# Attention of a two-layer hybrid backbone: values, gate and scores in halves of TensorE's array, channel by token

## The chip, the cores and the metric

One NeuronCore of a Trainium2 chip runs one program. The metric is the device time of one execution in microseconds, the median of several runs.

## The reference

A latent stream of 1024 tokens (8 tiles of 128) and a context of 256 tokens (2 tiles), both 1024 channels wide, in float32, pass two layers. A layer projects the modulated, normalised input into groups of channels, mixes each group in its own way, joins them through one output projection, and ends with routed experts. What the change touches:

```python
def spatial_gating(u, g, w_sgu, b_sgu):
    u = jax.nn.gelu(u, approximate=False)
    v = layer_norm(jax.nn.gelu(g, approximate=False))
    vh = v.reshape(b, n // SGU_CHUNK, SGU_CHUNK, N_SGU_HEADS, SGU_HEAD)
    mixed = jnp.einsum('hpq,bcqhd->bcphd', w_sgu, vh) + b_sgu.T[None, None, :, :, None]
    return u * mixed.reshape(b, n, GROUP_W)
...
    s_loc = jnp.einsum('bnikgd,bnjkd->bnkgij', qb, kw).astype(jnp.float32) * scale
    s_ctx = jnp.einsum('bnikgd,bckd->bnkgic', qb, kc).astype(jnp.float32) * scale
    probs = jax.nn.softmax(jnp.concatenate([s_loc, s_ctx, sink_l], axis=-1), axis=-1)
    o = (jnp.einsum('bnkgij,bnjkd->bnikgd', probs[..., :n_loc].astype(v.dtype), vw)
         + jnp.einsum('bnkgic,bckd->bnikgd', probs[..., n_loc:n_loc + n_ctx].astype(vc.dtype), vc))
...
    return jnp.concatenate([y_four, y_attn, y_pool, y_sgu], axis=-1) @ w_out
...
        x = layer_norm(RES_ALPHA * x + g1 * y, ln1_g[layer], ln1_b[layer])
        h2 = modulate(x, sh2, sc2)
```

There are 4 query heads of 64 channels on 2 key and value heads, and 4 gate heads of 64 channels. A tile of 128 queries sees three blocks of 128 keys (masked to +-128 tokens) and the 256 keys of the context; context tiles see the context alone. Each head has a sink logit in its softmax. `h2` goes to a router of 36 columns and to the experts. Layer 1 leaves the context's own output out.

## The kernel before

A layer runs in stages: `project_first` or `project_again` (input projection of 10 tiles, modulation vectors beside it), a transform stage (Fourier group and the like), `attend`, and `route_and_experts`. Tensors in SBUF written by one stage are read by the next: `qT` and `kT` channel by token, `v_tok`, `u_tok` and `sgu_v` token by channel, `four_tok` (in fact channel by token here) and `poolT` channel by token.

`attend` runs over its tiles as a software pipeline: in step t, tile t is attended, tile t-1 projected and tile t-2 routed. On TensorE (L1366 on, function `step`) the order of a step is: scores of pair 0 (two heads of one key head); the heads of tile t-1 turned from token by channel (`heads_tok`) to channel by token, 4 transposes (L1331), which ScalarE copies to `mixT` (L1245); first half of the projection of t-1 (512 of the 1024 output columns, 8 matmuls over 1024 channels, L1320); the probabilities of pair 0 turned, 10 transposes (L1290), copied by ScalarE to `probsT`; scores of pair 1; `h2` of t-2 turned, 8 transposes (L1347, L1350); second half of the projection; router of t-2 (L1360), whose result lies in the bank of `head_out`; values of pair 0 (L1305); probabilities of pair 1 turned; gate (L1311); values of pair 1.

A head of scores multiplies `q_head`, 128 rows of which the 64 of the other key head are zero, by 384 local keys (L1269) and 256 context keys (L1270). GpSimd makes `q_head` (L1085) by multiplying `qT` with a constant of ones and zeros, `K_KV`; it also copies the rows of `four_tok` and `poolT` into `mixT` (L1089, L1091), and computes the power for the norms (`norm_power`), the gain and bias behind the first norm (L1075, L1078) and the modulation of `h2` (L1099, L1101), each of 1024 elements per row.

Values have the turned probabilities as the stationary operand and 64 columns of `v_tok` moving, so `head_out` is token by channel; the gate has `w_sguT` stationary and 64 columns of `sgu_v` moving:

```python
mm = nc.tensor.matmul(O[:, 0, h * HD:(h + 1) * HD], pT[:, i, j, :], v, start=j == js[0], stop=j == 4)
...
nc.tensor.matmul(O[:, 1, h * HD:(h + 1) * HD], ws[:, h, :], sg[:, h * HD:(h + 1) * HD], start=True, stop=True)
```

VectorE masks scores and takes their maxima (`maxima`), normalises `h2` of t-2, copies it turned into `h2T` (L1180, L1182), adds the residual of t-1 once both halves of the projection are there (L1193, L1195), normalises that, and in `heads` adds `b_sgu`, multiplies by `u` (L1158) and divides the attention by its denominators (L1159), which are one number per token and so one per row. ScalarE takes the exponentials with their sums, copies turned tiles, and copies the router's logits (L1252). SyncE issues the stage's loads in the order of its code (`small_in` counts `b_sgu`, `w_sguT` and the two parts of `w_router`; TensorE waits for all four ahead of values of tile 0) and stores `h2`.

In the projection stages, the group u and g is 8 matmuls with `hT` stationary and 512 columns of `w_in` moving into `bankA`; ScalarE's gelu writes `u_tok` and `sgu_v`.

## Time and profile before

| | us |
|---|---|
| median of 3 runs | 2843.64 (2838.64 to 2847.23) |
| the profiled execution, its own time | 2844.69 |
| its span in the profile | 2842.5 |
| TensorE busy | 2454.1 (86%) |
| VectorE, ScalarE, GpSimd busy | 852.5 (30%), 437.3 (15%), 514.4 (18%) |
| attention, layer 0 (10 tiles) | 376.0 to 733.6 |
| attention, layer 1 (8 tiles) | 1757.4 to 2048.0 |
| input projection, layer 0 | 50 to 316 |
| mean granted clock of TensorE | 0.918 of full |

Times are microseconds from the start of the span. A matmul in float32 leaves two rows in the trace, a transpose one. Busy times of TensorE come with a modelled end: the start of the next row tells how long one really occupied the engine.

### The profile page before, as it was taken

To read this page: it belongs to the slowest core of one execution; us is meant where nothing else is said; L and a number is where in the kernel's file an instruction comes from. 1 tells how busy PE (TensorE), PEld (TensorE's weight loads), DVE (VectorE), ACT (ScalarE), POOL (GpSimd) and SP (SyncE) were. 2 spreads that over 40 slices of the span, in tenths; PEclk is the share of its full clock that TensorE was granted. 3 is DMA by queue.
4 is the path that set the end of the run, shared out by engine and by line. 5 is a ranking of instruction groups with operands and counts; after the bars stand their busy time and mean duration, and the time that the engine had idled before them with its cause. 6 is when DMAs were issued, how large, how long until landed. Compare 5 with 4: busy or idle time off the path is not lost. (4 is left out here: it accounts for less than half of the span.)

```text
span 2842.5 us, 38989 instructions
## 1 busy us (share of the span) xinstructions
PE 2454.1 (86%) x14774; PEld 1686.9 (59%) x14774; DVE 852.5 (30%) x2043; ACT 437.3 (15%) x1052; POOL 514.4 (18%) x691
## 2 busy tenths in 40 slices
PE   5999889998389999999967997999659999999960
PEld 3788556665266666666635784666346666666630
DVE  1232625543611111111107665454531111111107
ACT  0011122221001111111101112222001111111112
POOL 0000114334011111111110102234101111111116
PEclk7999889988589999999988998999769999999985
DMA  9444320001369999997534103000059999999953
GB/s 352 165 141 174 113 102 16 15 15 45 130 257 388 396 392 387 388 395 302 207 113 150 44 31 134 30 15 23 15 208 384 386 386 394 389 384 384 373 198 137
DMA packets 130588, 608.21 MB, mean 214 GB/s; under 512 B 21216, under 2 KB 23776, under 8 KB 112080
## 3 DMA queue, kind: packets, MB, share of 16 engines
q1 hardware_dynamic: 112048, 569.35, 51.6%
q0 software_dynamic: 17312, 37.79, 3.6%
q8 instruction: 50, 0.82, 0.1%
q14 instruction: 26, 0.21, 0.0%
q10 hardware_dynamic: 1152, 0.03, 0.0%
HBM read 612.52 MB, written 42.83 MB: 231 GB/s over the span
## 5 line engine op out<-in xcount | busy, mean ns | idle before, releaser
L1829 PEld LDWEIGHTS gate_up<-room,w_gate_up 128*128 128x128 f32 x4736 | 534.5, 193 | 32.3 <-issue 32.3
L1829 PE MATMUL gate_up<-room,w_gate_up 128*128 128x128 f32 x4736 | 541.6, 277 | 3.1 <-DVE room L1741 3.1
L1320 PE MATMUL proj<-w_out,mixT 128*128 128x512 f32 x576 | 261.7, 608 | 13.1 <-ACT mixT L1245 11.6
L1838 PE MATMUL down<-w_down,room 128*128 128x512 f32 x592 | 263.9, 599 | 0.0
L1846 PE MATMUL gate_up_short<-w_gate_up,room 128*64 128x512 f32 x1184 | 262.2, 595 | 0.0
L1750 DVE TENSOR_TENSOR room<-room,gate_up 128x128 f32<-128x128 f32 x148 | 42.6, 288 | 613.5 <-ACT room L1769 613.5
L1320 PEld LDWEIGHTS proj<-w_out,mixT 128*128 128x128 f32 x576 | 109.3, 195 | 142.7 <-issue 130.9
L1846 PEld LDWEIGHTS gate_up_short<-w_gate_up,room 128*64 128x64 f32 x1184 | 81.7, 137 | 175.9 <-issue 175.9
L1838 PEld LDWEIGHTS down<-w_down,room 128*128 128x128 f32 x592 | 109.4, 190 | 126.4 <-issue 123.9
L1753 DVE TENSOR_TENSOR room<-room,gate_up_short 128x256 f32<-128x256 f32 x37 | 15.6, 421 | 508.8 <-ACT room L1775 508.8
L1496 POOL COPY rows_idx<-slot_token 128x1 int32 (+1 forms) x80 | 14.6, 183 | 831.8 <-PE rows_turned L1816 729.7
L1859 PE MATMUL down<-w_down,room 128*64 128x512 f32 x592 | 135.2, 598 | 12.2 <-ACT room L1777 12.2
L1769 ACT ACTIVATE room<-gate_up 128x128 f32<-128x128 f32 x148 | 41.0, 277 | 519.8 <-PE gate_up L1829 519.8
L1816 PE MATMUL rows_turned<-consts,rows 128*128 128x128 f32 (+1 forms) x608 | 93.1, 286 | 17.7 <-DMA rows<-h_rows,rows_idx 17.7
L1816 PEld LDWEIGHTS rows_turned<-consts,rows 128*128 128x128 f32 (+1 forms) x608 | 77.1, 197 | 52.5 <-issue 48.0
L1741 DVE COPY room<-rows_turned 128x512 f32<-128x512 f32 (+1 forms) x152 | 78.2, 556 | 61.0 <-PE rows_turned L1816 61.0
L1305 PE MATMUL head_out<-v_tok,probsT 128*128 128x64 f32 (+1 forms) x672 | 89.8, 293 | 6.5 <-ACT logits L1252 6.5
L1499 POOL DMA_INDIRECT rows<-h_rows,rows_idx x80 | 80.9, 1012 | 71.7 <-POOL rows_idx L1496 50.1
L1305 PEld LDWEIGHTS head_out<-v_tok,probsT 128*128 128x128 f32 x672 | 86.6, 209 | 8.8 <-issue 8.6
L1859 PEld LDWEIGHTS down<-w_down,room 128*64 128x64 f32 x592 | 40.5, 136 | 81.3 <-issue 81.3
L467 PE MATMUL bankA<-w_in,hT 128*128 128x512 f32 x160 | 74.3, 619 | 15.9 <-ACT hT L412 15.9
L1773 ACT ACTIVATE room<-down 128x512 f32<-128x512 f32 x74 | 44.2, 597 | 267.0 <-PE down L1838 267.0
(322 smaller groups left out, 3039.6 us busy)
## 6 DMA issues: line engine op xcount, KB each, us to landing
w_gate_up<-in_w_exp_gate SPq DMA_DIRECT2D x74, 2048.0 KB, 8.8
w_gate_up<-in_w_exp_up SPq DMA_DIRECT2D x74, 2048.0 KB, 13.4
w_down<-in_w_exp_down SPq DMA_DIRECT2D x74, 2048.0 KB
ada_w<-in_w_ada SPq DMA_DIRECT2D x48, 1024.0 KB, 7.0
h_rows<-h SPq DMA_DIRECT2D x18, 512.0 KB, 2.6
w_out<-in_w_out SPq DMA_DIRECT2D x2, 4096.0 KB, 16.3
w_in<-in_w_in SPq DMA_DIRECT2D x2, 3072.0 KB, 16.6
xn<-expert_rows SPq DMA_DIRECT2D x10, 512.0 KB, 4.0
```

What stands on the lines that cost most here:

```text
L467: i = nc.tensor.matmul(out, lhsT(k), rhs(k), start=k == 0, stop=k == KT - 1)
L1305: mm = nc.tensor.matmul(O[:, 0, h * HD:(h + 1) * HD], pT[:, i, j, :], v, start=j == js[0], stop=j == 4)
L1320: mm = nc.tensor.matmul(Y[:, half, :], ys[1 - q][:, j, :], wo[:, k, half * 512:(half + 1) * 512], start=j == 0, stop=j == KT - 1)
L1499: pool.indirect_dma_start(xg[q][rows, :], None, g.h2[:, :], bass.IndirectOffsetOnAxis(ap=idx[q][rows, 0:1], axis=0), bounds_check=NT * P - ...
L1741: c = nc.vector.tensor_copy(xT[q][:, 4 * h:4 * h + 4, :], T[:, 4 * h:4 * h + 4, 0:P if q == 0 else HP])
L1750: nc.vector.tensor_tensor(hid[:, j, :], silu[:, j % 2, :], H[j % 2][:, 1, :], ALU.mult).then_inc(hid_done, 1)
L1773: nc.scalar.activation(yo[:, h * 512:(h + 1) * 512], Y[:, h, :], ACT.Copy).then_inc(y_done, 1)
L1816: tr = nc.tensor.transpose(T[:, k, 0:rows], xg[q][0:rows, k::KT], g.k[0:rows, K_ID:K_ID + rows])
L1829: mm = nc.tensor.matmul(H[j % 2][:, o, :], wgu[0][:, o, k, j * P:(j + 1) * P], xT[0][:, k, :], start=k == 0, stop=k == KT - 1)
L1838: mm = nc.tensor.matmul(Y[:, h, :], hid[:, j, :], wd[0][:, j, h * 512:(h + 1) * 512], start=j == 0, stop=j == JT - 1)
L1846: mm = nc.tensor.matmul(Hs[c * HP:(c + 1) * HP, :, :], xT[1][:, k, :], wgu[1][:, :, k, c * 2 * P:(c + 1) * 2 * P], start=k == 0, stop=k == ...
L1859: mm = nc.tensor.matmul(Y[h * HP:(h + 1) * HP, 0, :], hidT_s[:, j % 2, j // 2 * HP:(j // 2 + 1) * HP], wd[1][:, j, h * 512:(h + 1) * 512], ...
```

## The change

- **Values and gate, channel by token.** `v_tok` and `sgu_v` are now the stationary operands (64 columns of the array) and turned probabilities and `w_sguT` move, 128 columns. The result of a key head or of an even gate head goes to partitions 0 to 63 of `head_out`, that of the other to 64 to 127. Nothing turns the heads any more. Of the row of four blocks of `head_out`, 0 and 1 hold the two pairs, 2 and 3 first the gate and then the denominators.
- **Denominators as rows.** They now vary along the free axis, so GpSimd makes four diagonal matrices from the reciprocals (`den_diag`, `diagonals`), TensorE multiplies ones by them (`spread_den`), ScalarE copies that to `den_rows` and VectorE multiplies (`heads`).
- **Pairs.** A pair is now one query head of each key head (`sink`, `neg_max` and so on take every second head). The host orders rows of `w_out` to fit.
- **Scores in row halves.** Queries and keys of a key head are its own 64 rows of `qT` and `kT`; there is no `q_head` and no `K_KV`. A head's columns are 384 local and 128 "near" context keys into `scores`, and 128 "far" context keys into `scores_far`, in the order near 0, far 1, near 1, far 0, with a wait for far 1 ahead of far 0. The maxima take 512 and 128 columns of each head.
- **Projection.** It reads `four_tok` and `poolT` where they are, so `mixT` holds gate and attention rows alone; the waits for the gate and the attention rows stand ahead of their matmuls within the first half.
- **Residual in halves.** VectorE multiplies, adds and takes the statistics of columns 0 to 511 behind the first half of the projection, of the others behind the second.
- **Order.** On TensorE the gate comes ahead of the second half of the projection, `h2` is turned behind the probabilities of pair 1, and the router is last, into one of the two `turn` banks; which of the two banks each turning takes comes from a table. The loops over tiles are written out. SyncE's loads are in another order, `b_sgu` as rows in four loads, and `small_in` counts seven loads.
- **u, channel by token.** In the projection stages the 256 columns of u are 2 x 8 matmuls with `w_in` stationary and `hT` moving (128 columns), g is 8 of 256 columns, and gelu writes `uT`.

TensorE, one middle step of `attend`, before, from the turning of the heads on (the scores of pair 0 that stand ahead of it are the same four rows as those of pair 1; `x8` here is 8 matmuls, which the trace shows as x16):

```order
L1331 MATMUL turn_0<-consts,heads_tok 128x128 x4
L1320 MATMUL proj<-w_out,mixT_0 128x512 x8
L1290 MATMUL turn_0<-consts,probs_0 128x128 x10
L1269 MATMUL scores<-kT,q_head_0 128x384
L1270 MATMUL scores_ctx<-kcT,q_head_0 128x256
...
L1347 MATMUL turn_0<-consts,h_0_0 128x128 x4
L1350 MATMUL turn_0<-consts,h_0_0 128x128 x4
L1320 MATMUL proj<-w_out,mixT_0 128x512 x8
L1360 MATMUL head_out<-w_router,h2T 128x36 x8
L1305 MATMUL head_out<-v_tok,probsT 128x64 x10
L1290 MATMUL turn_0<-consts,probs_0 128x128 x10
L1311 MATMUL head_out<-sgu_v,w_sguT 128x64 x4
L1305 MATMUL head_out<-v_tok,probsT 128x64 x10
```

The same step now. `qT` as it is stands where `q_head` was, and operands of values and gate have changed places:

```order
L1276 MATMUL turn_0<-consts,probs_0 128x128 x10
L1259 MATMUL scores<-kT,qT 128x384
L1260 MATMUL scores<-kcT,qT 128x128
L1263 MATMUL scores_far<-kcT,qT 128x128
...
L1303 MATMUL head_out<-w_sguT,sgu_v 64x128 x4
L1324 MATMUL proj<-w_out,four_tok 128x512 x2
L1324 MATMUL proj<-w_out,poolT 128x512 x2
L1324 MATMUL proj<-w_out,mixT_0 128x512 x4
L1295 MATMUL head_out<-probsT_0,v_tok 64x128 x10
L1276 MATMUL turn_0<-consts,probs_0 128x128 x10
L1276 MATMUL turn_0<-consts,h_0_0 128x128 x8
L1310 MATMUL head_out<-den_diag,consts 64x128 x4
L1295 MATMUL head_out<-probsT_0,v_tok 64x128 x10
L1340 MATMUL turn_0<-w_router,h2T 128x36 x8
```

The four transposes of `heads_tok` are gone, the gate stands ahead of the second projection half, `h2` is turned behind the probabilities of pair 1, four rows of `den_diag` are new and the router is at the end.

SyncE at the start of `attend`, before:

```order
L1023 DMA sink<-in_attn_sink 128x4
L1024 DMA b_sgu<-in_b_sgu 128x4
L1025 DMA w_sguT<-in_w_sgu 128x512
L1020 DMA mod_0<-mods 128x1024 x3
L1027 DMA w_router<-in_w_router_group 128x8x4
L1028 DMA w_router<-in_w_router_expert 128x8x32
L1029 DMA w_out<-in_w_out 128x8x1024
L1031 DMA ln_0<-in_ln_g 128x1024
L1031 DMA ln_0<-in_ln_b 128x1024
```

SyncE now:

```order
L1013 DMA sink<-in_attn_sink 128x4
L1014 DMA w_sguT<-in_w_sgu 128x512
L1016 DMA b_sgu<-in_b_sgu 64x128 x4
L1017 DMA w_out<-in_w_out 128x8x1024
L1010 DMA mod_0<-mods 128x1024 x3
L1020 DMA ln_0<-in_ln_g 128x1024
L1020 DMA ln_0<-in_ln_b 128x1024
L1021 DMA w_router<-in_w_router_group 128x8x4
L1022 DMA w_router<-in_w_router_expert 128x8x32
```

The two parts of `w_router`, which `small_in` counts, have moved behind `w_out`, the vectors and the norm's gain and bias.

```diff
@@ project_first, TensorE and ScalarE (project_again alike) @@
-                    run(A[:, :], lambda k: h[:, k, :], lambda k: w[:, k, C_U:D_IN]).then_inc(a_done, 1)
+                    for j in range(2):
+                        run(A[:, j * P:(j + 1) * P], lambda k: w[:, k, C_U + j * P:C_U + (j + 1) * P], lambda k: h[:, k, :])
+                    run(A[:, GW:2 * GW], lambda k: h[:, k, :], lambda k: w[:, k, C_U + GW:D_IN]).then_inc(a_done, 1)
...
@@ attend, VectorE @@
+                def gate_out(t):
+                    out = ys[t % 2][:, 2:4, :]
+                    v.wait_ge(gate_full, t + 1)
...
+                    small(nc.vector.tensor_tensor(out, O[:, 2:4, :], bs[:, :, :], ALU.add))
+                    done()
+                    nc.vector.tensor_tensor(out, out, m.u[:, :, at_tile(t)], ALU.mult).then_inc(sgu_done, 1)
...
+                def heads(t):
+                    v.wait_ge(rb_read, t + 1)
+                    nc.vector.tensor_tensor(ys[t % 2][:, 0:2, :], O[:, 0:2, :], rb[:, :, :], ALU.mult).then_inc(o_ready, 1)
+
+                def residual(u, half):
+                    h, x = hb[u % 2][:, half * 512:(half + 1) * 512], g.x[:, u, half * 512:(half + 1) * 512]
...
+                    v.wait_ge((y0_full, y1_full)[half], u + 1)
+                    nc.vector.tensor_tensor(h, Y[:, half, :], vec[:, 0, half * 512:(half + 1) * 512], ALU.mult).then_inc(y_used, 1)
+                    v.wait_ge(y_used, 2 * u + half + 1)
+                    small(nc.vector.scalar_tensor_tensor(x, x, ALPHA, h, ALU.mult, ALU.add))
+                    done()
+                    nc.vector.memset(n1.spare[:, :], 0.0)
+                    small(nc.vector.bn_stats(n1.stats[:, half, :], x))
...
@@ attend, GpSimd @@
-                        i = nc.gpsimd.tensor_tensor(qs[q][:, 2 * kv:2 * kv + 2, :], m.qT[:, :, at_tile(t)], own_rows, ALU.mult)
...
-                    nc.gpsimd.tensor_copy(ys[q][:, 4:6, :], m.four[:, :, at_tile(t)])
...
+                def diagonals(t):
+                    pool.wait_ge(den_ready, t + 1)
+                    if t:
+                        pool.wait_ge(rb_full, t)
+                    nc.gpsimd.tensor_tensor(dg[:, :, :], across(g.k[:, K_ID:K_ID + P], NH), over(den[:, :], P), ALU.mult).then_inc(diag_ready, 1)
...
@@ attend, TensorE @@
+                    def near(i):
+                        if not is_ctx(t):
+                            nc.tensor.matmul(S[:, i, 0:BW], qh[i], m.kT[own[i], t * P:t * P + BW], start=True, stop=True)
+                        nc.tensor.matmul(S[:, i, BW:BW + P], qh[i], m.kcT[own[i], 0:P], start=True, stop=True)
+
+                    def far(i):
+                        return nc.tensor.matmul(SC[:, i, :], qh[i], m.kcT[own[i], P:2 * P], start=True, stop=True)
+
+                    near(0)
+                    far(1).then_inc(far_scored, 1)
+                    near(1)
+                    pe.wait_ge(far_scored, t * 2 + pair + 1)
+                    far(0).then_inc(scored, 1)
...
+                            mm = nc.tensor.matmul(O[kv * HD:(kv + 1) * HD, pair, :], m.v[:, block, kv * HD:(kv + 1) * HD], pT[pair][:, kv, j, :],
+                                                  start=j == js[0], stop=j == 4)
...
+                        mm = nc.tensor.matmul(O[h % 2 * HD:(h % 2 + 1) * HD, 2 + h // 2, :], m.sg[:, t, h * HD:(h + 1) * HD], ws[:, h, :], start=True, stop=True)
...
+                            mm = nc.tensor.matmul(O[kv * HD:(kv + 1) * HD, 2 + pair, :], g.k[:, K_ONE:K_ONE + HD], dg[:, 2 * kv + pair, :], start=True, stop=True)
...
+                    mix = ([(0, m.four[:, 0, at_tile(u)]), (1, m.four[:, 1, at_tile(u)]), (4, m.pT[:, 0, o:o + P]), (5, m.pT[:, 1, o:o + P])]
+                           + [(k, ys[u % 2][:, j, :]) for k, j in ((6, 2), (7, 3), (2, 0), (3, 1))])
```

## Rows read from the trace of the kernel before

**Rows 1.** Windows: time, busy of PE, PEld, DVE, ACT, POOL, PEclk, DMA share, GB/s
```profile
50.00:316.00 266.00, 262.12 (x2632) 209.69 (x2631) 72.47 (x255) 26.50 (x77) 13.29 (x36) 0.99 0.49 173
376.00:733.60 357.60, 313.44 (x1352) 209.70 (x1352) 160.28 (x366) 75.56 (x237) 123.65 (x118) 0.89 0.11 40
588.10:595.00 6.90, 6.90 (x35) 6.66 (x34) 2.71 (x9) 1.51 (x3) 3.87 (x4) 0.51 0.00 0
...
1757.40:2048.00 290.60, 251.34 (x1152) 167.25 (x1152) 134.61 (x308) 67.00 (x209) 95.47 (x93) 0.93 0.11 40
```

**Rows 2.** TensorE's timeline, a middle tile: start us, us, operation, count, [idle before <-releaser]
```profile
502.22 7.13 PE L1320 MATMUL proj<-w_out,mixT 128*128 128x512 f32 x16 [0.69 <-ACT mixT L1245]
...
510.75 0.81 PE L1269 MATMUL scores<-kT,q_head 128*128 x2
...
512.91 0.60 PE L1347 MATMUL turn<-consts,h 128*128 128x128 f32 x4
...
513.78 7.03 PE L1320 MATMUL proj<-w_out,mixT 128*128 128x512 f32 x16
520.65 1.87 PE L1360 MATMUL head_out<-w_router,h2T 128*128 128x36 f32 x16
523.00 2.42 PE L1305 MATMUL head_out<-v_tok,probsT 128*128 x20 [0.48 <-ACT logits L1252]
525.25 1.04 PE L1290 MATMUL turn<-consts,probs 128*128 128x128 f32 x8
...
526.82 1.00 PE L1311 MATMUL head_out<-sgu_v,w_sguT 128*128 x8
...
529.89 0.86 PE L1269 MATMUL scores<-kT,q_head 128*128 x2
...
532.78 0.65 PE L1331 MATMUL turn<-consts,heads_tok 128*128 128x128 f32 x4 [0.52 <-DVE heads_tok L1159]
```

**Rows 3.** The same view, both attention stages: first halves of the projection
```profile
409.25 7.10 PE L1320 MATMUL proj<-w_out,mixT 128*128 128x512 f32 x16 [0.73 <-issue]
...
437.91 7.13 PE L1320 MATMUL proj<-w_out,mixT 128*128 128x512 f32 x16 [0.69 <-ACT mixT L1245]
...
534.28 7.13 PE L1320 MATMUL proj<-w_out,mixT 128*128 128x512 f32 x16 [0.84 <-ACT mixT L1245]
...
636.80 7.13 PE L1320 MATMUL proj<-w_out,mixT 128*128 128x512 f32 x16 [0.69 <-ACT mixT L1245]
...
694.47 8.55 PE L1320 MATMUL proj<-w_out,mixT 128*128 128x512 f32 x16 [0.69 <-ACT mixT L1245]
...
1816.99 7.13 PE L1320 MATMUL proj<-w_out,mixT 128*128 128x512 f32 x16 [0.69 <-ACT mixT L1245]
...
2009.71 9.69 PE L1320 MATMUL proj<-w_out,mixT 128*128 128x512 f32 x16 [0.69 <-ACT mixT L1245]
```

**Rows 4.** The same view in the input projection of layer 0
```profile
74.90 1.95 PE L467 MATMUL bankD<-hT,w_in 128*128 128x128 f32 x16
76.78 1.93 PE L451 MATMUL ada_ps<-ada_w,cond_silu 128*2 128x128 f32 x64
78.64 7.13 PE L467 MATMUL bankA<-w_in,hT 128*128 128x512 f32 x16
```

**Rows 5.** Groups by form, attention of layer 0: busy, mean ns, idle before, releaser
```profile
L1101 POOL TENSOR_TENSOR h<-h,mod 128x1024 f32<-128x1024 f32 x9 | 21.1, 2349 | 0.7
...
L1085 POOL TENSOR_TENSOR q_head<-qT,consts 128x256 f32<-128x256 f32 x20 | 11.8, 612 | 22.4 <-POOLq L173 20.9 <-PE scores_ctx L1270 1.4
...
L1158 DVE TENSOR_TENSOR heads_tok<-heads_tok,u_tok 128x256 f32<-128x256 f32 x10 | 9.8, 984 | 0.8
...
L1180 DVE COPY h2T<-turn 128x512 f32<-128x512 f32 x10 | 6.9, 686 | 8.0 <-PE turn L1347 8.0
...
L1245 ACT ACTIVATE mixT<-turn 128x512 f32<-128x512 f32 x10 | 6.0, 597 | 64.8 <-PE turn L1331 64.8
```

**Rows 6.** DMA issues at the start of attention, layer 0: KB each, us to landing
```profile
w_out<-in_w_out SPq DMA_DIRECT2D x1, 4096.0 KB, 15.7
```

573 lines of the change are left out of this document (268 added, 305 removed).

## The prediction, made blind

> **What bounds the kernel now.** I read the windows by stage first [rows 1]. The two attention stages, which the change rewrites, last 357.6 and 290.6 us. TensorE is busy for 313.4 and 251.3 us of them, VectorE for 160.3 and 134.6, GpSimd for 123.7 and 95.5, and DMA is 11% busy. So TensorE bounds them, through its work and its waits. Next comes TensorE's timeline over one middle tile [rows 2], from one first half of the projection to the next: 534.28 - 502.22 = 32.06 us at a granted clock that is full (the same piece elsewhere repeats within half a microsecond). A run of rows, each starting where the last one ended, shows what a tile costs TensorE. Each float32 matmul leaves two rows: 8 of the projection are x16. Only four idle times stand in the tile that a reader should price: 0.25 us twice behind ScalarE's copies, 0.48 us behind the router's copy, and the excursion that turns the heads. That one runs from the end of the scores to the projection, and is 0.52 us of wait for heads_tok, 0.65 us of transposes and 0.84 us until the copy into mixT is made. The last scores start at 529.89 and take as long as the pair from 510.75 to 512.91, 2.16 us, so they end at 532.05, and the excursion is 2.2 us. Then come the starts of the projection over the stages [rows 3], which give the periods: 12 steady ones, 636.80 - 437.91 = 198.9 us in layer 0 and 2009.71 - 1816.99 = 192.7 in layer 1.
>
> **The steady tile, piece by piece.** (1) The excursion goes: values leave TensorE as channel rows already, so its 2.2 us leave the path. What is late next is the projection's first half, whose last two matmuls read the attention rows. They stand behind the next pair of scores, four matmuls that need nothing and two that need the gate, six at 6.87 / 8 = 0.86 us, 5.2 us; the heads need ScalarE's copy and a product of VectorE meanwhile, about 1 us, and are covered. **-2.2.**
> (2) Values. 20 rows per pair take 525.25 - 523.00 = 2.25 us, 0.112 each, 64 columns moving. Now they are 20 rows of 128 moving columns on half of the array's columns, two head groups alternating. That 64 moving columns already cost 0.112 lets me take 0.112 as the price of 128 too: bankD's 16 rows with 128 columns take 1.88 us, 0.117 each [rows 4], a switch of forms included. Column groups do run at once: the ada rows, 64 with 128 moving columns in four groups, take 78.64 - 76.78 = 1.86 us, 0.029 each, a quarter [rows 4]. So with two groups, half: 1.15 a pair. Twice, **-2.2**; if the halves don't pair, 0.
> (3) Gate: 8 rows, 1.00 us with its tail (0.16, as the projection's 7.03 against 6.87 to the next row's start), 0.84 without, become 0.45: **-0.4**. New is the spreading of the denominators, 8 rows of the same form: **+0.45** (0.9 unpaired).
> (4) Scores. A pair takes 2.16 us for 1280 columns in two rows each. The columns stay, but each head now sits on half of the array's rows. No row of this kernel shows row halves; the bounds are 1.1 us (all at once) and 2.2 (none). By the order of issue, only the 128 columns of "far" have another half's matmul ahead of them, so 2 x 0.215 us are hidden (by the projection: 6.87 us for 16 rows of 512, so 0.107 for 128 columns, twice): 1.75. Twice, **-0.8**, between -2.1 and 0.
> (5) The router keeps its 1.87 us (520.65 on). Its wait of 0.48 us for ScalarE goes with the shared bank. In its place it waits for VectorE's two copies of h2T, 0.69 us each [rows 5], and runs behind values; between 0 and 1.4, I take 0.45: **0**.
> (6) Forms. Four stretches per tile are now in halves (two scores, gate, values with spreading), so TensorE goes into and out of halves four times. From bankD into the ada rows there is 0.1 us: 16 rows at 0.112 are 1.79 us, and 76.78 - 74.90 is 1.88 [rows 4]; out again, into bankA, I allow twice that for want of a row. So 0.3 per excursion, between 0.1 and 0.65: **+1.2**.
> The sum is -2.2 - 2.2 - 0.4 + 0.45 - 0.8 + 1.2 = **-4.0 us per tile**, 28.1 for 32.06.
> The Trainium skill ("TensorEngine Tiling (Array Packing)", Key Properties) speaks against this change: changing the tiling mode drains TensorE. The ada rows agree that it isn't free, with 0.1 us; by the page alone the sum would be the same, for it names no price.
>
> **Other engines.** GpSimd loses two q_head products, 2 x 0.61 us [rows 5], and two copies, and gains one product of 128x512, by L1101's 2.35 us for 1024 elements about 1.2: a little lighter. ScalarE trades the mixT copy, 0.60 us [rows 5], for one of half the size. VectorE does the same work, the residual in halves: its first half now runs beside the second projection half, where VectorE idles. That moves some 2 us of it off the time behind the projection and onto the time beside it, and lets the norm behind the projection end sooner. What queues behind the first half on VectorE are the maxima of pair 1, which need turning and scores first, some 3 us (10 transposes and 1.75). Costed at nothing; the cover is VectorE's idle share, 54% of the stage [rows 1].
>
> **The whole.** Twelve periods at 28.1 are 337 us for 391.6: **-54.4**; this includes some 7 us by which these periods exceed 12 x 32.06 today, in stretches at a low granted clock (588.1 to 595 at 0.51 [rows 1]). I count them as gone, because TensorE's idle excursions go; if not, the forecast is 7 higher. The first periods, 437.91 - 409.25 = 28.7 and layer 1's, which I take as alike, have no router yet: -3.4 each, **-7**. The two context periods, 694.47 - 636.80 = 57.7 together, lose the heads' excursion, fewer values but the same gate: **-8**. The tails, from 694.47 to 733.6 and from 2009.71 to 2048.0, 38 to 39 us each, hold one projection and two routers: the residual in halves takes about 1 us off a chain of one tile, and the excursion is gone: -4 and -2.5, **-6.5**.
> Tile 0: its gate now waits for all small loads, w_router among them, which SyncE issues behind w_out and five broadcasts. VectorE's adding of the bias and, behind it, the denominators wait with it, and ScalarE and the heads for these. w_out is 4 MB and lands after 15.7 us [rows 6]; all loads of the stage are 7.2 MB, so by that row all lie there at the latest 27.6 us after 376, at 403.6, and gate, values, turning and scores need 6.5 us behind it, plus 1.5 for the heads: first projection at the latest 411.6, against 409.25. Between 0 and +5 per layer, I take 2: **+4**. The host's reordering of w_out costs nothing on the chip.
> The projection of u: 16 rows of 512 columns, bankA's 7.13 us less the tail of 0.16 [rows 4], 6.97, become 32 of 128 (0.112 to 0.117) and 16 of 256 (half the 0.43 of 512): 7.0 to 7.2 us. Eighteen tiles at 0.15: **+2.7**. This stage is TensorE's (262.1 busy of 266 us), so it counts in full.
> Sum: -54.4 - 7 - 8 - 6.5 + 4 + 2.7 = -69 us. The profiled execution took 2844.7 us, 1 us over the median of three, so 2844.7 - 69 = 2775.5, and 2775 against the median. What a measurement here can tell from no change is about 0.3%, 8.5 us.
>
> **The rivals.**
> *C, the row halves run at once.* Scores take 1.1 us instead of 1.75, and -1.3 per tile in 16 tiles makes -21: about 2755. For it: the four column groups did [rows 4]. Against: the order of issue, and one wait on a semaphore amid each pair. The Trainium skill ("TensorE: Matmul & The Clock Gate", Part 3, "What overlaps and what doesn't") has matmuls start and end strictly in program order, which forbids the full overlap; no row here shows it.
> *B, VectorE and GpSimd become the bound.* VectorE's product at L1158 averages 0.98 us for 256 elements where L1180's copy of 512 takes 0.69: it reads and writes SBUF alone, and I take it as stretched by GpSimd's products of 2.35 us [rows 5]. With periods 4 us shorter, more of VectorE's work falls beside GpSimd's, and the router or the scores wait for it, 1.2 us more per tile: +20, about 2795.
> *A, the halves don't pair (the change doesn't do what it says).* Values and scores keep their time, spreading costs 0.9, the forms 1.2, only the excursion goes: -2.2 + 0.9 + 1.2 = -0.1 per tile; with the 4 and 2.7 of tile 0 and u, about 2848, the same or a bit slower. Against it stand the ada rows.
> *D, slower: TensorE's clock stays low in the stretches in halves.* They are 3.5 + 2.3 + 0.45 + 0.45 = 6.7 us of 28.1. The granted clock fell to half at 588 us (from 2.4 to 1.2 GHz) although TensorE was 100% busy there [rows 1], so a high busy share does not guard it. If all four stretches ran at 1.2 GHz in all 16 tiles, that costs 6.7 x 16 = 107 us for the 69 saved: about 2883. It decides from 65% of them on; at 70% the result is 2850. Against: the ada stretches, in quarters of the array, ran in a stage whose granted clock is 0.99 [rows 1].
>
> **How the numbers follow.** The forecast has 0.62, B 0.15, C 0.12, A 0.06, D 0.05. Forecast, B and C are faster by more than 0.3%; A gives half same, half slower; D slower: faster 0.89, same 0.04, slower 0.07. The range goes from 2750 (C, with 0.2 for the forms' 0.3, another 6 us) to 2815 (B with the forms at 0.65, which adds 1.4 per tile, or 22, less what is rounded), and leaves out A and D.
>
> **What would show it.** Right: mid-layer periods between projection starts of 28 us; no transposes of heads; 20 rows of values in 1.15 us; scores of a pair in 1.75; gaps of 0.1 between forms; DVE named by router waits under 1 us. Wrong: values at 2.2 us (A), a period over 29 with DVE or POOL as the releaser of TensorE's waits (B), scores at 1.1 (C), PEclk below the 0.89 and 0.93 of the stages of before (D).

## The result, and the profile after

The changed kernel takes 2767.61 us (median of 4 runs, 2765.92 to 2770.49), the kernel before 2845.43 us (median of 4 by now, 2838.64 to 2856.37): a ratio of 0.972, with a 95% interval of 0.970 to 0.974. The profiled execution has a span of 2765.6 us, 76.9 less than before.

The windows of the two attention stages after, with the columns of [rows 1]:

```profile
382.60:693.60 311.00, 271.35 (x1472) 169.07 (x1472) 165.08 (x406) 75.21 (x253) 117.44 (x88) 0.91 0.13 46
1716.30:1973.90 257.60, 222.19 (x1248) 140.63 (x1248) 138.68 (x332) 65.23 (x209) 90.83 (x69) 0.92 0.12 46
```

They last 311.0 and 257.6 us for 357.6 and 290.6, by these bounds. The next window runs from the second first half of the projection to the eighth in layer 0, six steady periods, first after, then before:

```profile
442.80:606.46 163.66, 159.08 (x934) 98.84 (x933) 99.64 (x246) 47.94 (x156) 75.89 (x56) 1.00 0.05 20
```

```profile
437.91:636.80 198.89, 188.63 (x860) 128.91 (x860) 95.10 (x232) 49.49 (x157) 77.05 (x73) 0.93 0.04 16
```

163.66 us for 198.89. TensorE's busy time is 159.1 us for 188.6, its idle time went from 10.3 to 4.6 us, and the granted clock is full where it was 0.93. So all three shrank: work, waits and the stretches at the lower clock.

TensorE's timeline over a middle tile after, against [rows 2]:

```profile
497.57 1.98 PE L1324 MATMUL proj<-w_out,four_tok 128*128 128x512 f32 x4
...
504.54 1.04 PE L1276 MATMUL turn<-consts,probs 128*128 128x128 f32 x8
...
506.26 0.59 PE L1259 MATMUL scores<-kT,qT 64*128 64x384 f32 x1
506.27 0.49 PE L1263 MATMUL scores_far<-kcT,qT 64*128 64x128 f32 x2
506.59 0.81 PE L1259 MATMUL scores<-kT,qT 64*128 64x384 f32 x3
507.00 0.62 PE L1260 MATMUL scores<-kcT,qT 64*128 64x128 f32 x4
507.46 0.48 PE L1263 MATMUL scores_far<-kcT,qT 64*128 64x128 f32 x2
507.88 0.66 PE L1303 MATMUL head_out<-w_sguT,sgu_v 128*64 128x128 f32 x8
508.46 1.98 PE L1324 MATMUL proj<-w_out,four_tok 128*128 128x512 f32 x4
...
515.53 1.31 PE L1295 MATMUL head_out<-probsT,v_tok 128*64 128x128 f32 x20
516.77 1.09 PE L1276 MATMUL turn<-consts,probs 128*128 128x128 f32 x8
...
518.75 1.06 PE L1276 MATMUL turn<-consts,h 128*128 128x128 f32 x8
519.75 0.66 PE L1310 MATMUL head_out<-den_diag,consts 128*64 128x128 f32 x8
520.24 1.26 PE L1295 MATMUL head_out<-probsT,v_tok 128*64 128x128 f32 x20
521.43 1.98 PE L1340 MATMUL turn<-w_router,h2T 128*128 128x36 f32 x16
523.33 0.59 PE L1259 MATMUL scores<-kT,qT 64*128 64x384 f32 x1
...
524.95 1.98 PE L1324 MATMUL proj<-w_out,four_tok 128*128 128x512 f32 x4
```

The period is 524.95 - 497.57 = 27.38 us, for 32.06. Five of the six periods of each layer repeat it within 0.02 us; the last, beside a context tile, is 26.7 us in layer 0 and the last of layer 1 is 25.7. Start to start, each piece against the one of before:

| piece | before | after | moved | forecast |
|---|---|---|---|---|
| excursion that turned the heads | 2.23 | 0 | -2.2 | -2.2 |
| values, two pairs | 4.48 | 1.24 + 1.19 | -2.05 | -2.2 |
| gate | 0.84 | 0.58 | -0.26 | -0.4 |
| spreading of denominators | | 0.49 | +0.49 | +0.45 |
| scores, two pairs | 4.32 | 1.62 x 2 | -1.1 | -0.8 |
| router and its wait | 2.35 | 1.90 | -0.45 | 0 |
| turning of probabilities and h2 | 4.00 | 1.72 + 1.98 + 1.00 | +0.7 | none; 0.3 is a wait |
| both halves of the projection | 13.84 | 6.97 + 7.07 | +0.2 | in the forms |
| sum | 32.06 | 27.38 | -4.7 | -4.0 |

The forecast's +1.2 for the forms has no row of its own: what entering and leaving halves costs lies at the edges of the pieces, in the last two rows and within values, gate and scores. But 0.3 us of the turning is a wait that the busy time hides, because the ends of TensorE's rows are modelled. The last two transposes of the probabilities start at 518.17 and 518.34, a transpose follows another after 0.11, and `h2` starts at 518.75. It goes into the bank that the second four turned probabilities had, and ScalarE's copy of these ends at 518.61:

```profile
518.02 0.59 ACT L1233 ACTIVATE probsT<-turn 128x512 f32<-128x512 f32 x1
```

Tile 0 of layer 0 after, rows of TensorE around its longest wait:

```profile
382.64 0.56 PE L1259 MATMUL scores<-kT,qT 64*128 64x384 f32 x1 [1.26 <-PEq L170]
...
407.80 1.12 PE L1303 MATMUL head_out<-w_sguT,sgu_v 128*64 128x128 f32 x8 [12.19 <-DMA w_router<-in_w_router_expert]
418.33 1.98 PE L1324 MATMUL proj<-w_out,four_tok 128*128 128x512 f32 x4
```

From the first scores to the first projection it is 418.33 - 382.64 = 35.7 us, for 409.25 - 377.22 = 32.0 before (36.3 for 30.1 in layer 1). TensorE sat idle for 12.2 us ahead of the gate, until the second part of w_router had landed (11.5 us in layer 1). The granted clock of this whole stretch is 0.62: values of pair 0 take 2.34 us here, from 410.07 on, and 1.24 in the steady tile. GpSimd in the same stretch:

```profile
404.46 2.78 POOL L1040 TENSOR_SCALAR mod<-mod 128x1024 f32<-128x1024 f32 x1 [43.92 <-DMA mod<-mods]
410.56 1.04 POOL L1059 TENSOR_TENSOR den_diag<-consts,denominator 128x512 f32<-128x512 f32 x1 [3.32 <-DVE denominator L1128]
```

The vector it adds one to lands only at 404.46, and the first diagonals come behind that and behind VectorE.

The projection of u in the input projection, against the bankA row of [rows 4]:

```profile
81.59 3.84 PE L464 MATMUL bankA<-hT,w_in 128*128 128x128 f32 x32
...
88.72 5.40 PE L464 MATMUL bankB<-w_in,hT 128*128 128x256 f32 x32
```

u and g together take 88.72 - 81.59 = 7.13 us for 6.97, and 7.03 for 6.87 in layer 1.

### The profile page after: what moved, and what is told of

It reads as the page before. It is cut to its first block and busy times, and to the rows that moved or that the text cites. A ratio compares the mean times of both kernels' runs of the same rounds, so it can differ in the third digit from the quotient of the medians.

```text
span 2765.6 us, 39991 instructions
## 1 busy us (share of the span) xinstructions
PE 2383.3 (86%) x15566; PEld 1685.6 (61%) x15566; DVE 859.5 (31%) x2107; ACT 435.0 (16%) x1068; POOL 504.3 (18%) x637
## 5 line engine op out<-in xcount | busy, mean ns | idle before, releaser
L1856 PE MATMUL down<-w_down,room 128*64 128x512 f32 x592 | 135.2, 598 | 12.2 <-ACT room L1774 12.2
L1324 PE MATMUL proj<-w_out,mixT 128*128 128x512 f32 x288 | 129.5, 592 | 0.0
L1324 PEld LDWEIGHTS proj<-w_out,mixT 128*128 128x128 f32 x288 | 54.7, 190 | 68.9 <-issue 68.9
L1507 POOL DMA_INDIRECT expert_rows<-room,y_idx x37 | 37.6, 1017 | 230.2 <-ACT room L1770 230.2
L464 PE MATMUL bankC<-hT,w_in 128*128 128x128 f32 x640 | 74.1, 277 | 0.0
L1324 PE MATMUL proj<-w_out,four_tok 128*128 128x512 f32 x144 | 74.0, 638 | 0.0
```

The lines of the kernel that those rows point to most:

```text
L464: i = nc.tensor.matmul(out, lhsT(k), rhs(k), start=k == 0, stop=k == KT - 1)
L1324: mm = nc.tensor.matmul(Y[:, half, :], rows, wo[:, k, half * 512:(half + 1) * 512], start=j == 0, stop=j == KT - 1)
L1856: mm = nc.tensor.matmul(Y[h * HP:(h + 1) * HP, 0, :], hidT_s[:, j % 2, j // 2 * HP:(j // 2 + 1) * HP], wd[1][:, j, h * 512:(h + 1) * 512], ...
```

## The experiments

Twelve kernels ran, each once unless the table says otherwise. "Period" is from one first half of the projection to the next, mid-layer in layer 0; it depends neither on what the experts do nor on how the start of the span falls. Single totals differ by some 5 us for the latter reason alone: the first scores started at 382.64 us in the profile of the change and between 376.2 and 380.1 in those of the experiments, which differ from it only later. So the readings below rest on periods and rows.

| run | period us | first scores to first projection, layers 0 and 1 | total us |
|---|---|---|---|
| before | 32.06 | 32.0, 30.1 | 2845.4 (4 runs) |
| the change | 27.38 | 35.7, 36.3 | 2767.6 (4 runs) |
| own_wait | 27.38 | 31.1, 31.3 | 2757.4 |
| own_wait_late_add | 27.38 | 25.9, 26.4 | 2747.1 (4 runs) |
| unpaired | 28.79 | | 2786.4 |
| serial_scores | 28.21 | | 2777.1 |
| alternate_scores | 27.36 | | 2765.4 |
| far_first | 26.72 | | 2755.3 |
| split_gate | 27.73 | | 2771.5 |
| whole_residual | 27.53 | | 2765.5 |
| gate_by_values | 29.7 | | 2797.7 |
| no_turning_of_heads | 30.8 | | other work for the experts |
| best_far_first | 26.72 | 24.8, 25.0 | 2731.8 (4 runs) |
| best_all | 28.0 to 29.2 | 27.2, 28.1 | 2772.4 (4 runs) |

### Tile 0: which load is late

```diff
-                        pe.wait_ge(small_in, 112)
+                        pe.wait_ge(small_in, 80)
...
+                    if u == 0:
+                        pe.wait_ge(router_in, 32)
```

The same bound of 80 stands on VectorE, and the two loads of w_router count on router_in.

> Question: the change's term for tile 0 (I took +2 us a layer; the trace shows first projections 35.7 and 36.3 us after the first scores, 32.0 and 30.1 before). Here the gate and the bias wait only for their own five loads, w_router has a semaphore of its own, awaited ahead of the first router; nothing else differs. If the gate's idle time of 12.2 us (layer 0) and 11.5 us (layer 1) behind the load of w_router is the cause: the gate of tile 0 starts right behind the scores of pair 1, and the next thing in the way is GpSimd, which adds one to a modulation vector that lands at 404.5 us (2.8 us) before it makes the first diagonals: first projection about 7.5 us earlier in layer 0 and 7 in layer 1, about 15 us in all. Rival: the other loads (w_out, landed 14.6 us after its issue) set the pace anyway: less than 3 us in all.

```profile
392.27 0.66 PE L1303 MATMUL head_out<-w_sguT,sgu_v 128*64 128x128 f32 x8
396.33 2.40 PE L1295 MATMUL head_out<-probsT,v_tok 128*64 128x128 f32 x20 [3.40 <-DVE mixT L1118]
...
404.57 1.12 PE L1310 MATMUL head_out<-den_diag,consts 128*64 128x128 f32 x8 [3.41 <-POOL den_diag L1059]
```

The gate's wait is gone, as expected, but only 4.6 and 5.0 us of the 7.5 and 7 came. The values of pair 0 now wait 3.4 us for VectorE's gate rows, and the spreading 3.4 us for the diagonals. GpSimd is in the way next, as expected, and so is a wait ahead of values that I had left out. The second kernel also moves GpSimd's addition:

```diff
-                add_one(0)
                 for t in range(N + 2):
...
                         diagonals(t)
+                    if t == 0:
+                        add_one(0)
```

> As the run before, and GpSimd adds one to the vector behind the first diagonals, not ahead of them. If the diagonals are what is late there, the first projection moves by another 3.5 us a layer, about 11 us earlier per layer than in the change and about 21 us in all, near 2746. If nothing but the probabilities of pair 1 is late (their exponentials end 400.9 us), there is no difference from the run before. Steady periods stay at 27.4 us in both.

```profile
398.52 2.50 PE L1277 MATMUL turn<-consts,probs 128*128 128x128 f32 x10
400.94 1.12 PE L1311 MATMUL head_out<-den_diag,consts 128*64 128x128 f32 x8
...
404.83 1.98 PE L1325 MATMUL proj<-w_out,four_tok 128*128 128x512 f32 x4
```

The spreading follows the turning without a wait; the first projection comes 9.8 and 9.9 us earlier than in the change (11 expected), and 5 us earlier than in the run before (3.5 expected). The total falls to 2747.13 us, 20.5 less than the change (21 expected), ratio to the kernel before 0.966 (0.964 to 0.968). So tile 0 cost some 10 us in each layer, by the order of loads and of GpSimd's program, and w_out held nothing up in either run. The 3.4 us of wait for VectorE's gate rows are still there in the second run.

### Is it the pairing of column halves?

```diff
-                    for j in js:
-                        block = t + j if j < 3 else LT + 2 + j - 3
-                        for kv in range(NKV):
+                    for kv in range(NKV):
+                        for j in js:
+                            block = t + j if j < 3 else LT + 2 + j - 3
...
-                    for h in range(NH):
+                    for h in (0, 2, 1, 3):
```

and the same exchange of loops in the spreading.

> Question: is it the pairing of two column halves that made values, gate and spreading short? Same instructions, but all matmuls of one key head (or of even gate heads) are issued before those of the other, so that neighbours sit on the same 64 columns. Theory (halves run at once only where neighbours are on different halves): 20 rows of values take 2.2 us instead of 1.24, the gate 0.9 instead of 0.58, spreading 0.9 instead of 0.49, so the period grows by 2 x 1.0 + 0.35 + 0.4 = 2.7 us, from 27.4 to about 30.1. Rival (the array sees ahead, or a row with 64 stationary columns is cheap by itself): the period stays within 0.5 us of 27.4.

```profile
480.72 0.67 PE L1303 MATMUL head_out<-w_sguT,sgu_v 128*64 128x128 f32 x8
481.31 1.98 PE L1324 MATMUL proj<-w_out,four_tok 128*128 128x512 f32 x4
...
488.38 2.02 PE L1295 MATMUL head_out<-probsT,v_tok 128*64 128x128 f32 x20
490.32 1.09 PE L1276 MATMUL turn<-consts,probs 128*128 128x128 f32 x8
```

The period grows by 1.41 us, half of what I expected. Values take 1.94 us for 1.24, but the gate keeps its 0.59. The starts of the single rows tell why:

```
values of pair 0, starts of rows, us
first half of the columns   488.375 488.535 488.644 488.753 488.862 488.971 489.081 489.190 489.299 489.408
second half                 489.086 489.246 489.356 489.465 489.574 489.683 489.792 489.901 490.011 490.120
gate
first half of the columns   480.716 480.876 480.986 481.095
second half                 480.730 480.890 480.999 481.108
```

The assignment to halves is my reading, by the program's order of issue and the pace of 0.109 us; the trace itself does not name the half. Read so, TensorE starts a matmul on the free half ahead of three rows that were issued before it for the busy half: the one of 489.190 and its two successors here, and in the gate those of 480.876 to 481.095. The overtaking row starts right behind the first row of the matmul that is two ahead of it (5 ns in the values, 14 in the gate). serial_scores, below, shows the same where the trace does name the matmuls. A gate of four rows a half is short enough to pair itself in this order; ten rows a half are not. Pairing is therefore what makes the values short (a row alone still takes 0.109 us). My theory had no look-ahead; the rival did ("the array sees ahead") but without a limit. The truth lies between them: values need the order, gate and spreading do not.

### The scores in row halves

serial_scores issues a head whole, then the other:

```diff
                     near(0)
-                    far(1).then_inc(far_scored, 1)
+                    far(0).then_inc(far_scored, 1)
                     near(1)
                     pe.wait_ge(far_scored, t * 2 + pair + 1)
-                    far(0).then_inc(scored, 1)
+                    far(1).then_inc(scored, 1)
```

> Question: what do the row halves give in the scores? A pair takes 1.62 us now, 2.16 before. Here the order is near 0, far 0, near 1, far 1 (each head whole, one after the other), the rest as it was. If only neighbours on different halves overlap, the pair takes about 2.0 (one boundary between heads is left), and the period grows by 2 x 0.4 = 0.8 us to 28.2. If the halves hardly overlap and the gain of 0.54 has another cause, the pair stays at 1.6 to 1.7.

The pair takes 2.04 us and the period 28.21, as expected. The one boundary between heads is seen here by the line numbers:

```profile
504.31 0.59 PE L1259 MATMUL scores<-kT,qT 64*128 64x384 f32 x1
...
504.52 0.38 PE L1263 MATMUL scores_far<-kcT,qT 64*128 64x128 f32 x2
```

The local matmul of the second head starts ahead of far 0, which was issued before it. Then the other way, always alternating:

```diff
+                    local(0)
+                    local(1)
+                    far(0).then_inc(far_scored, 1)
+                    near(1)
+                    pe.wait_ge(far_scored, t * 2 + pair + 1)
+                    far(1).then_inc(scored, 1)
+                    near(0).then_inc(scored, 1)
```

> Question: how far can row halves overlap? The order is local 0, local 1, far 0, near 1, (wait for far 0) far 1, near 0: neighbours always sit on different halves of the rows, with 384, 384, 128, 128, 128, 128 columns. If halves run fully at once, a pair takes 1280 columns in two rows each on one half, 1.1 us and some 0.1 for the wait, and the period falls by 2 x 0.4 us to 26.6. If matmuls start and end strictly in order, so that the pass of one half holds up the other's, the pair stays at 1.6 and the period at 27.4.

```profile
503.71 0.92 PE L1259 MATMUL scores<-kT,qT 64*128 64x384 f32 x4
...
504.57 0.27 PE L1265 MATMUL scores_far<-kcT,qT 64*128 64x128 f32 x1
...
504.90 0.37 PE L1265 MATMUL scores_far<-kcT,qT 64*128 64x128 f32 x1
```

The period stays (27.36), which is what the rival said, but not for its reason. Rows of both halves start together: far and near lie 7 ns apart in each couple of matmuls. Between the last start of the first couple of 128 columns, 504.57, and the first of the second, 504.90, are 0.33 us where 0.11 is the pace: there stands the program's wait for far 0 ahead of far 1, which writes the same bank. The next kernel puts that couple first:

```diff
+                    far(0).then_inc(far_scored, 1)
+                    near(1)
                     local(0)
                     local(1)
-                    far(0).then_inc(far_scored, 1)
-                    near(1)
                     pe.wait_ge(far_scored, t * 2 + pair + 1)
```

> Question: the run with alternating scores kept 1.61 us a pair; is that because halves cannot overlap more, or because of the wait for far 0? In its trace the 384-column rows of both halves start within 7 ns of each other, and 0.33 us lie between the last row of far 0 and the first of far 1, where 0.11 is the pace. Here the order is far 0, near 1, local 0, local 1, (wait for far 0, long done) far 1, near 0. Theory: the pair falls by the 0.22 us of the wait, to about 1.4, and the period from 27.4 to 26.9. Rival: a waiting matmul is an ordering point by itself, whatever it waits for (0.1 to 0.2 us): 1.5 to 1.6, period 27.1 to 27.4.

```profile
500.16 0.37 PE L1265 MATMUL scores_far<-kcT,qT 64*128 64x128 f32 x1
...
500.48 0.81 PE L1259 MATMUL scores<-kT,qT 64*128 64x384 f32 x4
501.13 0.27 PE L1262 MATMUL scores<-kcT,qT 64*128 64x128 f32 x1
...
501.45 0.66 PE L1307 MATMUL head_out<-w_sguT,sgu_v 128*64 128x128 f32 x8
```

The waiting couple now starts without a gap, and the pair takes 501.45 - 500.16 = 1.29 us (1.4 expected, 1.62 in the change). The period is 26.72. So row halves overlap wholly where neighbours are on different halves and nothing waits between them: each half has 640 columns in two rows each, 1.07 us at 0.107 for 128, and the rest is entering and leaving. A wait that is already met costs nothing here. The 0.1 us that I had not expected was behind the wait: in alternate_scores the second row of the waiting far 1 came 0.21 us after the first (504.898, 505.111), and here 0.11.

### What a change of forms costs

split_gate puts two of the four gate matmuls behind the fourth matmul of the second half of the projection:

```diff
+                        if half == 1 and j == 4 and att(u + 1):
+                            gate(u + 1, (2, 3))
...
-                        gate(t)
+                        gate(t, (0, 1) if t else (0, 1, 2, 3))
```

> Question: what does one more way into halves and out again cost? The gate's matmuls of heads 2 and 3 stand amid the second half of the projection (behind its fourth matmul) instead of with heads 0 and 1: same work, one more excursion per tile. I forecast 0.3 us per excursion. By that the period goes from 27.4 to 27.7. If a change of form costs 0.65 each (the rival that made the change slower), it goes to 28.7; if it is free, it stays, within 0.1.

```profile
508.03 0.44 PE L1303 MATMUL head_out<-w_sguT,sgu_v 128*64 128x128 f32 x4
508.40 3.70 PE L1327 MATMUL proj<-w_out,mixT 128*128 128x512 f32 x8
```

27.73 us: one more excursion costs 0.35 us, 0.3 forecast. Four rows, two per half, would be 0.22 us, and 508.40 - 508.03 is 0.37. So 0.15 us lies within the stretch itself, and 0.2 in the rows around it.

### The residual in halves

The two calls stand together where the second was:

```diff
-                    if prj(t):
-                        residual(t - 1, 0)
                     if att(t):
                         maxima(t, 1)
...
                     if prj(t):
+                        residual(t - 1, 0)
                         residual(t - 1, 1)
```

> Question: does the residual in halves give anything? Both halves are done where the second is now, behind the second half of the projection. The router's rows start without any wait now. VectorE's chain behind the projection (multiply, add, statistics, norm, then the copies of h2) grows by the first half's 0.69 + 0.69 + 0.69 = 2.1 us. If the slack at the router is smaller than that, TensorE waits there and the period grows by up to 2 us (I expect 0.5 to 1.5); if the halves only moved idle time, it stays at 27.4 and only the tails grow, by 2 us each.

27.53 us, 0.15 more. In the change, VectorE stands idle for 1.77 us ahead of the second half's residual, and its copies of h2T end 0.46 us before the router starts (519.69 + 1.28 = 520.97, 521.43):

```profile
515.64 0.69 DVE L1144 TENSOR_TENSOR h<-proj,mod 128x512 f32<-128x512 f32 x1 [1.77 <-PE proj L1324]
...
519.69 1.28 DVE L1181 COPY h2T<-turn 128x512 f32<-128x512 f32 x2
```

And in whole_residual, where values of pair 0 start at 511.73 (515.53 in the change):

```profile
512.37 0.67 DVE L1144 TENSOR_TENSOR h<-proj,mod 128x512 f32<-128x512 f32 x1
...
516.41 1.28 DVE L1181 COPY h2T<-turn 128x512 f32<-128x512 f32 x2
```

The first half's residual ran in that idle time, from 509.99 on. So the chain behind the projection grew by 0.5 us (512.37 - 511.73 = 0.64 us, for 0.11), not by the 2.1 that I expected, and used up the slack of 0.46 us at the router. In the steady tile the halves are worth 0.15 us, and costing them at nothing was right. Of the last steps of a layer, where the forecast gave them about 1 us, the run says nothing: nothing is attended there, and the edit leaves VectorE's order as it was.

### One excursion less

The gate moves behind the second half of the projection, next to the values, into the free half of the bank of scores_far. The waits follow the banks.

```diff
                     if prj(t):
                         project_half(t - 1, 1)
                     if att(t):
+                        gate(t)
                         values(t, 0)
...
-                        mm = nc.tensor.matmul(O[h % 2 * HD:(h % 2 + 1) * HD, 2 + h // 2, :], ...
+                        mm = nc.tensor.matmul(SC[h % 2 * HD:(h % 2 + 1) * HD, 2 + h // 2, :], ...
```

> Question: can one excursion per tile be saved, as split_gate added one for 0.35 us? The gate stands behind the second half of the projection, right ahead of values of pair 0 (both on column halves), in the free half of the bank of scores_far, so that VectorE can read it while values are written to the other bank. If a change of forms is what costs, the period falls from 27.4 by 0.15 to 0.35. Rival: gate_out and the denominators now come behind the projection on VectorE, 1.6 us ahead of the residual, the norm and h2's copies, so the router or the spreading waits; whole_residual delayed that chain by 2.1 us and lost 0.15. By that the period stays within 0.1 or grows.

The period is 29.7 us (89.10 over three), 2.3 more. The end of a step on TensorE, and the windows around it:

```profile
520.02 1.26 PE L1297 MATMUL head_out<-probsT,v_tok 128*64 128x128 f32 x20
522.64 1.95 PE L1341 MATMUL turn<-w_router,h2T 128*128 128x36 f32 x16 [1.36 <-DVE h2T L1181]
```

```profile
497.51:524.00 26.49, 24.37 (x142) 14.74 (x141) 16.79 (x41) 7.80 (x25) 10.12 (x10) 1.00 0.05 21
524.00:527.20 3.20, 3.20 (x18) 2.70 (x17) 0.00 (x0) 0.20 (x1) 2.20 (x1) 0.61 0.00 0
```

The rival happened, and dearer than priced. VectorE works 1.3 us on gate rows and denominators between the projection and its residual, and h2T is complete 7.7 us after the end of the projection, for 5.4 in the change. The slack at the router was 0.46 us, and so the router waits 1.36 us. The granted clock is still full over the first 1.4 us of the router's rows and 0.61 from 524.0 to 527.2, at 1.2 GHz for most of it: the pair of scores takes 2.70 us for 1.62, 1.1 us more. Gate and values together did get shorter, 1.68 us for 1.82, and 1.36 + 1.08 - 0.14 is the 2.3 lost. So it was VectorE's 1.3 us that I had underpriced, by taking the slack of whole_residual for 2 us.

### The excursion of the heads alone

In the kernel before, without the transposes of the heads, their copy and their waits (the projection reads zeros for the attention and gate rows, so that only the time in the stage can be compared):

```diff
-                        pe.wait_ge(e.o_ready, t)
-                        pe.wait_ge(e.pt_free, t * 6)
-                        for j in range(4):
-                            tr = nc.tensor.transpose(T[0][:, j, :], os[:, j // 2, j % 2 * P:(j % 2 + 1) * P], ident)
-                        tr.then_inc(e.o_turned, 1)
...
-                        nc.scalar.activation(ys[1 - q][:, 0:4, :], T[0][:, :, :], ACT.Copy).then_inc(e.o_free, 1)
```

> Question: what was the excursion of the heads worth in the kernel before? This is the kernel before without the four transposes of the heads, their copy to mixT and the waits that belong to them; the attention and gate rows of mixT are zeros, so these two groups are left out of the projection. Theory (my first term, -2.2 us per tile): the period of 32.06 us falls to 29.9. Rival (the wait hides something that comes late next, such as the scores waiting for q_head or VectorE's maxima): it falls by less than 1 us. The total is not comparable, since other tokens go to other experts; the periods are.

The period is 30.8 us (464.24, 495.10, 525.87 us are starts of first halves), not 29.9. 0.9 us of the 2.2 comes back as a new wait, which stands in this row:

```profile
506.62 0.65 PE L1334 MATMUL turn<-consts,h 128*128 128x128 f32 x4 [0.77 <-POOL h L1101]
```

GpSimd's second product on h2 ends 4.9 us after its norm, and TensorE now arrives at the turning of h2 before it. In the change this wait does not exist: h2 is turned behind the probabilities of pair 1, half a tile later. So the new order of the step, which I had costed at nothing, goes with the whole 2.2 us; that is read from the two timelines, as no run has the change with h2 in its old place.

In layer 1 of this run the periods were 31.7 to 36.8 us, with the clock low again:

```profile
1904.40:2073.00 168.60, 161.50 (x693) 111.97 (x692) 76.49 (x187) 38.28 (x125) 61.92 (x56) 0.88 0.04 16
```

Taking the excursion out did not by itself keep the clock up: layer 0 had it full from 464.24 to 587.76, layer 1 did not, with nearly the same waits in each tile.

### The best of both

> The late add and the own wait of tile 0 (2747.1) with the scores of far_first. If the two gains add, by 16 tiles x 0.5 us if the pair is at 1.4: about 2739. If the scores stay at 1.6: 2747.

2731.8 us (2727.9 to 2735.0, 4 runs), 0.958 of the kernel before (0.956 to 0.961), and 35.8 us less than the change. Alone the two edits gave 20.5 and 12.3 us (far_first, one run), so the gains add, and a little more. The scores gave more than expected, since the pair takes 1.29 and not 1.4.

> The run before with the gate ahead of values. If the excursion saved gives 0.25 us a tile: 4 us less, about 2735. If VectorE's chain takes it back: 2739 or more.

2772.4 us (2771.1 to 2774.4), 40.6 more than without that edit: VectorE's chain takes it back, and as in gate_by_values part of the clock (0.98 over the steady periods for 1.00).

## Why the prediction was right

2775 was forecast, within 2750 to 2815; 2767.6 came. Against the profiled execution, with 2842.5 - 2765.6 = 76.9 us of span in place of 69:

| term | forecast | measured |
|---|---|---|
| twelve steady periods | -54.4 | -65.4 |
| first periods | -7 | -8.0 |
| context periods | -8 | -6.6 |
| tails | -6.5 | -7.1 |
| tile 0, both layers | +4 | +9.9 |
| projection of u | +2.7 | +2.3 |
| all else (start of the span, transform, experts, end) | 0 | -2.0 |

The mechanism was right in its main terms, and the total is closer than its terms: the steady periods gave 11 us more than forecast and tile 0 took 5.9 back, which is luck. Of the 11, some 8.6 are the 0.7 us per tile that is accounted for below, and 2.4 are the last of the six periods of each layer, which are shorter than the rest.

- **The excursion, -2.2.** The rows bear it out. no_turning_of_heads shows that in the old order of the step it is worth 1.2 alone; that the new order keeps the rest is read from the timelines.
- **Values, -2.2: -2.05.** The ada rows were the right ones to read it from [rows 4]: halves do run at once. unpaired shows the pairing as the cause for the values; gate and spreading pair in either order.
- **Scores, -0.8: -1.1.** The value taken, 1.75 us, was too high and its reason wrong. I took the order of issue as strict and hid only the far columns. In the timeline after, far 1 (L1263) starts at 506.27, while the context matmul of near 0 (L1260), issued ahead of it, starts no earlier than 507.00; in serial_scores it is 504.31 against 504.52. Rival C (1.1 us) describes what the array can do; the change's own order keeps it at 1.62, and far_first reaches 1.29. The Trainium skill ("TensorE: Matmul & The Clock Gate", Part 3) says that matmuls start and end in program order; for rows on different halves, starts do not.
- **Forms, +1.2.** One excursion costs 0.35 by split_gate, 0.3 forecast. The Trainium skill ("TensorEngine Tiling (Array Packing)", Key Properties) says that changing the tiling mode drains TensorE. The 0.35 us is what going in and out costs in this kernel; whether it is a drain, the trace does not tell.
- **A wait left out, +0.3.** `h2` waits for the bank of the turned probabilities, as shown under the table of pieces. The sum had nothing for it.
- **Router, 0: -0.45.** The wait I put in, 0.45 us for h2T, did not come: h2T is complete 0.46 us early. This and the excess of the scores, 0.28, make the difference of 0.7 per tile; the other rows cancel out.
- **The clock.** That the stretches at a low clock would go was right, 0.93 to 1.00 over the steady periods of layer 0. My reason, the idle excursions, is not shown. For it speaks gate_by_values, where one edit brings an idle time of 1.36 us per tile and low stretches with it. Against it speak no_turning_of_heads, whose layer 1 is at 0.88 without the excursion, and the stretch at 588.1 [rows 1] itself: it began 0.6 us behind TensorE's wait of 0.48 us for ScalarE (the values of that tile start at 587.54), some 21 us behind the turning of the heads. The cause stays open. Rival D did not occur: halves ran at full clock in the steady periods of both layers (1.00 from 1777.03 to 1939.61 too). By its sign alone it would seem to, as layer 1's whole stage is at 0.92 for 0.93; but the low stretches lie in tile 0 (0.62) and behind the last projection (0.77). The row that D rested on shows TensorE busy during a low stretch, not what it did before the clock fell.
- **Tile 0, +4: +9.9.** This is the term that was mis-sized. The bound on the landing of w_router, 403.6 or 26.4 us after the first scores of the old kernel, held: it landed 25.2 and 25.4 us after the first scores of the new one, at 407.8 in layer 0, since those started 5.4 us late. But I then took 2 us out of a range of 0 to 5 although the load came near its bound, and the path behind it took 10.5 us (407.80 to 418.33) for the 8.0 that I had counted, part of it at the low clock. Worse, I compared with the old first projection of 409.25, as if the new kernel had no reason to be earlier. Without the wait, and with GpSimd's addition behind the diagonals, the new tile 0 needs only 25.9 us. The right comparison was with the path of the new kernel, and the loss against it is 10 us in each layer.
- **Rival B** (VectorE and GpSimd bound) did not occur: TensorE waits 0.3 us three times per tile, each time for ScalarE. gate_by_values shows how near it is, with 0.46 us of slack at the router.

## What to carry to other kernels

Where matmuls use 64 of 128 rows or columns, put neighbours in the program on different halves, and place any wait that two of them need of each other where it has long been met. When a path gets shorter, price each load against the new path and not against the old finishing time: the 10 us a layer lost at tile 0 were in the order of the loads and of GpSimd's program. And before moving work onto a chain, read its slack where the two paths meet, and not from what another edit cost: whole_residual lost only 0.15 us because its work fell into idle time, and gate_by_values, which found 0.46 us of slack for 1.3 us of work, lost 2.3 us and part of the clock.

## What the runs showed of the hardware

- Matmuls on different halves of the array start out of program order; "nothing reorders the instructions", in the section on the kernel before, does not hold for them. Four rows a half paired fully though issued half by half (gate in unpaired, 0.59 us); of ten rows, three were overtaken (489.086 against 489.190 to 489.408). In each of these places, and at 504.306 in serial_scores, the overtaking row started 5 to 14 ns behind the first row of the matmul two ahead of it, here 489.081, 480.716 and 504.300.
- Two row halves run wholly side by side: 1.29 us for a pair with 1.07 us of columns (far_first), 2.16 us on the full array (before).
- A wait met long before cost nothing (501.13 in far_first); one not yet met cost 0.22 us ahead of the waiting row (504.90 in alternate_scores) and 0.1 behind it.
- One way into halves and out again costs 0.35 us (split_gate).
- The granted clock was 0.61 from 524.0 to 527.2 in gate_by_values, 1.4 us and more behind an idle time of 1.36 us, and stayed at 1.00 through the six steady periods of the change, whose listed idle times are of 0.31 us. It also fell without such an idle time before it (588.1 in the kernel before, behind one of 0.48).
